# Ordering the experts by token count and halving the rows of fifteen of them in a fused transformer kernel

## The reference, cut to what matters

```
logits = hf @ router_w + router_b            # 512 x 32
top_val, top_idx = top_k(logits, 4); gate = softmax(top_val)
# every (token, expert) pair becomes a row of its expert's block(s) of 128 rows
u = hf[toks] @ w1[e] + b1[e]                 # 1024 -> 2048
g_ = minimum(u[:, :1024], 7);  lin = clip(u[:, 1024:], -7, 7)
y = ((lin + 1) * g_ * sigmoid(1.702 * g_)) @ w2[e] + b2[e]
out[token] += y * gate                       # four rows for each token
```

## Time and profile before

| | |
|---|---|
| device time, median of 3 runs | 3612.74 us (3610.33 to 3614.78) |
| span of the profiled execution | 3608.3 us |
| what lies around the span, against the median | 4.4 us |
| PE busy / DVE / ACT / GpSimd, share of the span | 93% / 80% / 39% / 20% |
| DMA, mean over the span | 307 GB/s |
| main steps of the expert stage | 30, about 498 to 1587 us of the span |

### The profile page before, as it was taken

The page is one execution under the profiler, slowest core; times in us unless marked ns, Lnnn a source line. Parts: engine busy times, 40 slices in busy tenths (PEclk is TensorE's granted clock), DMA queues, the critical chain, the costliest instruction groups (busy, mean ns, idle before and its releaser), DMA issues. The chain is left out here.

```text
span 3608.3 us, 39584 instructions
## 1 busy us (share of the span) xinstructions
PE 3345.7 (93%) x13996; PEld 2292.9 (64%) x13996; DVE 2896.8 (80%) x4756; ACT 1400.6 (39%) x1740; POOL 715.6 (20%) x720
## 2 busy tenths in 40 slices
PE   7999999999999999999999999988888888888876
PEld 4878767878787777775877787644443444434432
DVE  5777689999999999995995474688888888888886
ACT  2235357777777777773232452111111111111110
POOL 0001000000000000001000100244444444444442
PEclk9999999999999999999999999999999999999999
DMA  7422189999999999994224113899999999999998
GB/s 274 161 83 100 35 322 372 372 381 371 383 370 382 369 384 369 384 371 173 95 82 140 47 50 116 339 401 421 421 417 415 414 411 408 422 420 407 415 421 343
DMA packets 253815, 1105.96 MB, mean 307 GB/s; under 512 B 21137, under 2 KB 30737, under 8 KB 187793
## 3 DMA queue, kind: packets, MB, share of 16 engines
q1 hardware_dynamic: 166322, 521.20, 39.7%
q0 software_dynamic: 80640, 562.07, 38.0%
q10 hardware_dynamic: 6720, 20.97, 1.4%
HBM read 1071.15 MB, written 33.03 MB: 306 GB/s over the span
## 5 line engine op out<-in xcount | busy, mean ns | idle before, releaser
L1796 DVE TENSOR_TENSOR moe_w_lo<-ring,moe_w_hi 128x2048 fp32r<-128x2048 f32 x383 | 859.3, 2286 | 37.9 <-ACT moe_w_hi L1704 37.9
L1704 ACT ACTIVATE moe_w_hi<-ring 128x2048 fp32r<-128x2048 f32 x380 | 706.5, 1913 | 107.2 <-DMA ring<-in_exp_w 78.2
L2538 PE MATMUL last_banks<-last_rows_b,ring 128*128 128x512 f32 x1024 | 510.2, 646 | 121.7 <-DVE ring L2738 121.5
L2538 PE MATMUL last_banks<-last_rows_a,ring 128*128 128x512 f32 x1024 | 476.5, 609 | 85.4 <-DVE ring L2738 85.1
L2630 ACT ACTIVATE last_gelu<-last_dot 128x2 f32<-128x2 f32 (+1 forms) x257 | 52.3, 203 | 1118.9 <-DVE last_dot L2735 1118.8
L2538 PEld LDWEIGHTS last_banks<-last_rows_b,ring 128*128 128x128 f32 x1024 | 201.5, 205 | 403.5 <-issue 216.1
L2538 PEld LDWEIGHTS last_banks<-last_rows_a,ring 128*128 128x128 f32 x1024 | 188.6, 193 | 327.4 <-issue 201.1
L2417 POOL DMA_INDIRECT last_rows_a<-in_peer_uv,last_ids x256 | 279.9, 1093 | 501.2 <-PE last_banks L2538 318.7
L2417 POOL DMA_INDIRECT last_rows_b<-in_peer_uv,last_ids x256 | 294.9, 1152 | 390.2 <-PE last_banks L2538 365.5
L1550 POOL COPY moe_col<-slots 128x1 uint32 x31 | 51.4, 1658 | 959.7 <-PE moe_tp L1578 959.7
L2738 DVE TENSOR_SCALAR ring<-consts_sb,last_gelu,last_gates 128x128 f32<-128x128 f32 x512 | 161.6, 387 | 76.9 <-ACT last_gelu L2630 76.0
(11 more groups left out here) (506 smaller groups left out, 6530.5 us busy)
## 6 DMA issues: line engine op xcount, KB each, us to landing
ring<-in_exp_w SPq DMA_DIRECT2D x384, 1024.0 KB, 7.3
ring<-in_w_in SPq DMA_DIRECT2D x38, 1024.0 KB, 5.4
...
y_rows<-spare SPq DMA_DIRECT2D x1, 7680.0 KB, 25.4
...
```

Source lines behind the costliest of these rows:

```text
L1704: nc.scalar.activation(w_hi[:, slot, :], env.ring[:, slot, :], ACT.Copy).then_inc(hi_done, 1)
L1796: nc.vector.tensor_tensor(w_lo[:, slot, :], env.ring[:, slot, :], w_hi[:, slot, :].bitcast(F32), ALU.subtract).then_inc(lo_done, 1)
L2538: last = nc.tensor.matmul(sums(t)[:, q, :], diag[:, n % SL], slot(n)[:, D + q * W:D + (q + 1) * W], start=first, stop=final)
```

## The change

Experts are ordered by row count in the chip's routing code. Expert 0 keeps place 0; the others are ranked, and places 0, 2, 4, ..., 30 and 31 (17 of them) get the largest, places 1, 3, ..., 29 (15 of them, "small") the smallest. `expert_at` holds the expert of each place, and SyncE reads it to address the weights. A small place holds 64 rows; an expert with more there would overflow to the extra blocks. The half of each small block of `y_rows` that nothing writes is filled from `x` beforehand.

For a small expert, the 64 rounded rows and the 64 rests stand side by side as one stationary operand of 128 columns (`xt_hi_b`, `hidt_hi`), so that hi and lo rows are done by one pass: 8 matmuls for a chunk in place of 12. PSUM then has the rounded rows' sums in partitions 0 to 63 and the rests' in 64 to 127. To add them, ACT copies the bank to SBUF (`g_part`, `l_part`, `y_part`) and PE adds it back, shifted by 64 partitions, with 2 matmuls by `to_first`. The rests times `w_lo`, which were left out before, are computed too.

The gate is done in three DVE passes: ACT's sigmoid reads the unclipped PSUM bank, DVE computes min(g, 7) * sigmoid in one pass from PSUM, the 1 of (lin + 1) is added to the bias beforehand, and the product is bounded by `GATED_MAX`.

The order of chunks in a step from a small to a full expert becomes g, l, y; from a full to a small one it stays g, y, l. The first and the last main step stand outside the loop, which runs 14 times.

In the routing stage (SyncE's fill, then DVE), and SyncE's loads in the expert stage:

```diff
+unused = m["y_dram"][0:N_EXP * P, :].rearrange("(g f r) n -> f g r n", f=4, r=HALF)[3]
+some_rows = d["x"].rearrange("(g r) n -> g r n", r=HALF)
+for g0, g1 in ((0, 8), (8, N_EXP // 2 - 1)):
+    sp.dma_start(unused[g0:g1], some_rows[0:g1 - g0]).then_inc(filled, 16)
...
+chain(nc.vector.scalar_tensor_tensor(tie[:], cps, float(N_EXP), tie[:], ALU.mult, ALU.add))
+chain(nc.vector.tensor_tensor(before_it[:], tie[:].unsqueeze(1).to_broadcast([P, N_EXP, N_EXP]), tie[:].unsqueeze(2).to_broadcast([P, N_EXP, N_EXP]), ALU.is_gt))
+chain(nc.vector.tensor_reduce(order[:], before_it[:], AX, ALU.add))
+chain.also(nc.vector.tensor_scalar(nb[:], cps, float(P), None, ALU.is_gt))
+chain.also(nc.vector.tensor_scalar(small[:], order[:], N_FULL - 0.5, None, ALU.is_gt))
+chain(nc.vector.tensor_scalar(base[:], order[:], N_FULL - 1.5, -float(P), ALU.is_gt, ALU.mult))
+chain.also(nc.vector.scalar_tensor_tensor(limit[:], cps, float(HALF), small[:], ALU.is_gt, ALU.mult))
+chain(nc.vector.scalar_tensor_tensor(base[:], order[:], float(2 * P), base[:], ALU.mult, ALU.add))
 for j in range(2, NT):
     chain(nc.vector.scalar_tensor_tensor(nb[:], cps, float(j * P), nb[:], ALU.is_gt, ALU.add))
+chain.also(nc.vector.scalar_tensor_tensor(base[:], small[:], -float(N_EXP * P), base[:], ALU.mult, ALU.add))
+chain(nc.vector.tensor_tensor(nb[:], nb[:], limit[:], ALU.add))
+chain.also(nc.vector.tensor_scalar(limit[:], small[:], -float(HALF), float(P), ALU.mult, ALU.add))
...
+chain.also(nc.vector.tensor_tensor(past[:], rps, wide(limit), ALU.is_ge))
 chain(nc.vector.tensor_tensor(over[:], bend[:], nb[:], ALU.subtract))
+chain(nc.vector.tensor_tensor(over[:], over[:], small[:], ALU.add))
...
+chain(nc.vector.tensor_tensor(at_place[:], base[:].unsqueeze(1).to_broadcast([P, N_EXP, N_EXP]), starts[:].unsqueeze(2).to_broadcast([P, N_EXP, N_EXP]), ALU.is_equal))
+chain(nc.vector.tensor_tensor(at_place[:], at_place[:], iota[:, 0:N_EXP].unsqueeze(1).to_broadcast([P, N_EXP, N_EXP]), ALU.mult))
+chain(nc.vector.tensor_reduce(expf[:], at_place[:], AX, ALU.add))
+chain(nc.vector.tensor_copy(m["expert_at"][:], expf[:]))
+chain(nc.vector.tensor_scalar(m["row_pick"][:, 0:N_EXP], expf[:], env.const("expert_of_row"), None, ALU.is_equal))
...
+    e_now, e_next = expert(i), expert(i + 1)
     for j, (kind, n) in enumerate(kinds):
         sp.wait_ge(used, 12 * i + j + 1)
-        load_chunk(env, sp, i + 1 if kind != "y" else i, kind, n, slot_of(par, j), landed)
...
+        load_chunk(env, sp, e_next if kind != "y" else e_now, kind, n, slot_of(par, j), landed)
```

On PE:

```diff
+def few_chunk(s, slot, n, both, bank):
+    pe.wait_ge(lo_done, s + 1)
+    for a in range(2):
+        k = 2 * n + a
+        for w in (w_hi, w_lo):
+            for q in range(2):
+                last = nc.tensor.matmul(bank[:, q, :], both[:, k, :], w[:, slot, a * D + q * W:a * D + (q + 1) * W],
+                                        start=k == 0 and w is w_hi, stop=k == KC - 1 and w is w_lo)
+    last.then_inc(used, 1)
+def add_part(part, bank):
+    for q in range(2):
+        last = nc.tensor.matmul(bank[:, q, :], to_first[:], part[:, q * W:(q + 1) * W], start=False, stop=True, skip_group_check=True)
+    return last
...
+def to_small(i, n_small, first=False):
+    b = i + 1
     pe.wait_ge(x_lo, b * 2 + 2)
     pe.wait_ge(glu_done, b)
     for j in range(4):
-        chunk(at(i, j), slot_of(par, j), j, xt[u], glu_ps)
+        few_chunk(at(i, j), slot_of(0, j), j, xt[1][0], glu_ps)
         if j == 1:
+            if not first:
+                pe.wait_ge(y_parted, n_small)
+                add_part(y_part, yp).then_inc(y_done, 1)
             turn_hidden(i)
     pe.wait_ge(pick_ready, b + 1)
-    bias(glu_ps, u, 0).then_inc(g_done, 1)
     pe.wait_ge(h_lo, b * 2)
     pe.wait_ge(y_moved, b)
     for j in range(4):
-        chunk(at(i, 4 + j), slot_of(par, 4 + j), j, hidt, yp)
+        chunk(at(i, 4 + j), slot_of(0, 4 + j), j, hidt, yp)
         if j == 0:
             turn_rows(b + 1)
+        if j == 1:
+            pe.wait_ge(g_parted, n_small + 1)
+            bias(glu_ps, 1, 0, True)
+            add_part(g_part, glu_ps).then_inc(g_done, 1)
     pe.wait_ge(lin_done, b)
     for j in range(4):
-        chunk(at(i, 8 + j), slot_of(par, 8 + j), j, xt[u], lin_ps)
-    bias(lin_ps, u, FF).then_inc(l_done, 1)
+        few_chunk(at(i, 8 + j), slot_of(0, 8 + j), j, xt[1][0], lin_ps)
+def from_small(i, n_small, few_next=True):
+    b = i + 1
+    pe.wait_ge(x_lo, b * 2 + 2)
+    pe.wait_ge(glu_done, b)
+    for j in range(4):
+        chunk(at(i, j), slot_of(1, j), j, xt[0], glu_ps)
+        if j == 1:
+            pe.wait_ge(l_parted, n_small + 1)
+            bias(lin_ps, 1, FF, True)
+            add_part(l_part, lin_ps).then_inc(l_done, 1)
+    pe.wait_ge(pick_ready, b + 1)
+    bias(glu_ps, 0, 0).then_inc(g_done, 1)
+    pe.wait_ge(lin_done, b)
+    for j in range(4):
+        chunk(at(i, 4 + j), slot_of(1, 4 + j), j, xt[0], lin_ps)
+        if j == 0:
+            turn_few_hidden(i)
+        if j == 1 and few_next:
+            turn_few_rows(b + 1)
+    bias(lin_ps, 0, FF).then_inc(l_done, 1)
+    pe.wait_ge(h_lo, b * 2)
+    pe.wait_ge(y_moved, b)
+    for j in range(4):
+        few_chunk(at(i, 8 + j), slot_of(1, 8 + j), j, hidt[0], yp)
+        if j == 0 and not few_next:
+            turn_rows(b + 1)
```

On ACT:

```diff
+def glu_part(b, chunks):
+    act.wait_ge(used, chunks)
+    act.wait_ge(glu_done, b)
+    nc.scalar.activation(g_part[:], flat(glu_ps), ACT.Copy).then_inc(g_parted, 1)
+def lin_part(b, chunks):
+    act.wait_ge(used, chunks)
+    act.wait_ge(h_turn, b * 2)
+    nc.scalar.activation(l_part[:], flat(lin_ps), ACT.Copy).then_inc(l_parted, 1)
+def rows_part(b, chunks):
+    act.wait_ge(used, chunks)
+    act.wait_ge(stored, b * 16 + 16)
+    nc.scalar.activation(y_part[:], flat(yp), ACT.Copy).then_inc(y_parted, 1)
+def few_rows_out(b, n_small):
+    act.wait_ge(y_done, n_small + 1)
+    nc.scalar.activation(y[0:HALF], flat(yp, HALF), ACT.Copy).then_inc(y_moved, 1)
+    act.wait_ge(y_moved, b + 2)
+    act.dma_start(y_dram[span(b * P, HALF), :], y[0:HALF]).then_inc(stored, 16)
...
+def to_small(i, eights, n_small, first=False):
 
     b = i + 1
     for j in range(12):
-        round_chunk(slot_of(par, j), (three + (8 + 12 * par + j) // SL + 1) * 16)
...
+        round_chunk(slot_of(0, j), (eights + (8 + j) // SL + 1) * 16)
+        if j == 2 and not first:
+            rows_part(i - 1, at(i, 0))
+        if j == 4:
             round_hidden(i)
+            if not first:
+                few_rows_out(i - 1, n_small - 1)
+        if j == 6:
+            glu_part(b, at(i, 4))
         if j == 8:
+            round_rows(b + 1, 0)
+        if j == 9:
+            gate_of(b, HALF)
+    rows_out(i, at(i, 8))
+def from_small(i, eights, few_next=True):
+    b = i + 1
+    for j in range(12):
+        round_chunk(slot_of(1, j), (eights + (20 + j) // SL + 1) * 16)
+        if j == 2:
+            lin_part(i, at(i, 0))
+        if j == 7:
+            round_few_hidden(i)
             gate_of(b)
-            round_rows(b + 1, par)
...
+        if j == 9 and few_next:
+            round_few_rows(b + 1)
```

On DVE:

```diff
-def clip_glu(b):
...
-    nc.vector.tensor_scalar(glu[:], glu_ps[:].rearrange("p q n -> p (q n)"), 7.0, None, ALU.min).then_inc(glu_done, 1)
...
-def gate_glu(b):
+def gate_glu(b, rows=P):
     dve.wait_ge(sig_done, b + 1)
-    nc.vector.tensor_tensor(glu[:], glu[:], sig[:], ALU.mult).then_inc(gated, 1)
...
+    nc.vector.scalar_tensor_tensor(glu[0:rows], flat(glu_ps, rows), GLU_MAX, sig[0:rows], ALU.min, ALU.mult).then_inc(glu_done, 1)
+def hidden(b, rows=P):
     dve.wait_ge(l_done, b + 1)
-    nc.vector.tensor_scalar(lin[:], lin_ps[:].rearrange("p q n -> p (q n)"), 7.0, -7.0, ALU.min, ALU.max).then_inc(lin_done, 1)
+    nc.vector.tensor_scalar(lin[0:rows], flat(lin_ps, rows), GLU_MAX + 1.0, 1.0 - GLU_MAX, ALU.min, ALU.max).then_inc(lin_done, 1)
     dve.wait_ge(lin_done, b + 1)
...
-    nc.vector.scalar_tensor_tensor(lin[:], lin[:], 1.0, glu[:], ALU.add, ALU.mult).then_inc(hid_done, 1)
...
+    dve.wait_ge(glu_done, b + 1)
+    nc.vector.scalar_tensor_tensor(lin[0:rows], glu[0:rows], GATED_MAX, lin[0:rows], ALU.min, ALU.mult).then_inc(hid_done, 1)
...
+def to_small(i, first=False):
 
     b = i + 1
...
+    pick_row(b, 1, HALF)
     for j in range(12):
-        rest_of_chunk(at(i, j), slot_of(par, j))
...
+        rest_of_chunk(at(i, j), slot_of(0, j))
+        if j == 0 and first:
             hidden(i)
...
+        if j == 4:
             rest_of_hidden(i)
...
-            clip_glu(b)
         if j == 8:
...
+            rest_of_rows(b + 1, 0)
+        if j == 10:
+            gate_glu(b, HALF)
+def from_small(i, few_next=True):
+    b = i + 1
+    pick_row(b, 0)
+    for j in range(12):
+        rest_of_chunk(at(i, j), slot_of(1, j))
+        if j == 3:
+            hidden(i, HALF)
+        if j == 7:
+            rest_of_few_hidden(i)
+        if j == 8:
             gate_glu(b)
+        if j == 9 and few_next:
```

(39 more changed lines are left out.)

150 lines of the change are left out of this document (98 added, 52 removed).

## The result

The changed kernel takes 3532.38 us (median of 4 runs, 3523.86 to 3535.16) against 3613.25 us (4 runs, 3610.33 to 3614.78): ratio 0.9768, 95% interval 0.9757 to 0.978, 80.9 us less. The forecast was 3560, in a range of 3522 to 3612; the direction and the bound hold, and the gain is 28 us larger than forecast. The profiled execution took 3535.16 us, its span is 3533.3: 1.9 us lie around the span, as in every run that lists both. The 4.4 us in the table of the kernel before are not that; its profiled execution, of span 3608.3, thus took near 3610.2, faster than its median.

The account below looks back on a forecast made before the run. PE was taken as the bound before, DMA after: 15 pairs of steps from 72.4 to 68.2 us save 63 us, the head adds 10.7, so -52.5 from 3612.7 gives 3560 us; range of 8 in 10, 3522 to 3612.

Parts of the forecast that it names:

- PE: Expert stage, matmul engine: bound of the kernel before; one small and one full expert fall from 72.4 to 62.6 us.
- DVE: Expert stage, vector passes: two steps fall from 67.8 to 64.3 us through two passes and two 512-column instructions fewer.
- DMA: Expert stage, loads, gathers and stores: 67.9 us for two steps (67.0 to 68.7), largest sum, taken as 68.2.
- the disturbance of the 128-row gather: Queues behind each full gather: 285 in place of 414 GB/s for 5.5 us, a cost of 1.7 us.
- slow stretch of half the length behind the small gather: Sign in the steady steps: after a 64-row gather the queues slow for half as long; disturbance taken as 0.85 us.
- GpSimd's index copy: Index copy beside the experts: 1.66 us on the mean, and 0.18 at its first, read as with DVE idle.
- ACT: Expert stage: three bank copies of 1.03 us added, 55.8 of 68.2 us for two steps; no cost taken.
- Head: Routing ahead of the experts: 8.7 us more serial DVE work and 2 for PE's low clock, +10.7 in sum.
- The list of signs: What the trace should show, including gathers 68.2 us apart and the first expert matmul 9 us later in the span.
- A: Rival: loads already at their ceiling of 377 GB/s, so only saved bytes count; 10 us less, 3602; chance 0.13.
- B: Rival: DMA gives way and DVE bounds the expert stage at 66.3 us a pair; 80 less, 3532; chance 0.22.
- C: Rival: ACT's in-order part copies stall the roundings, 79.2 us a pair; slower, 3725; chance 0.12.

Follow-up runs that it names:

- The first run: The kernel before with the three-pass gate alone, no ordering and no 64-row blocks: 3607.61 us, ratio 0.9996 against the kernel before.

## Why the prediction was right, and where it was off

**PE.** Right: the bound goes away from PE. 63.6 us a pair against 62.6; 42 matmuls fewer a pair, as counted. Where the 1.0 us more comes from isn't shown.

**DVE.** Right: 64.2 against 64.3. Its 1.9 us below the pair are no cost, as the run with a pass less shows; but 2.35 us of DVE more cost 2.65 a pair. The first run shows the other side, nothing saved under a busy PE. With PE 63.6, DVE 64.2 and DMA 66.1 the three limits stand close together: relief for PE alone gave 3.8 us of the 6.3 a pair, and the gate paid only with it.

**DMA.** The bound as forecast, and the term that was mis-sized. 26.74 MB a pair at 411 GB/s is 65.1 us; 411 is the mean rate from 12 to 20 us behind the 128-row gathers of the kernel after, well clear of them. I had added 1.7 us for the disturbance of the 128-row gather, 0.85 for the 64-row one and 0.3 for DVE; measured is 66.09 - 65.1 = 1.0 for all of it. The step that failed is the reading of the earlier trace rows: I took 285 GB/s over 5.5 us as the price of the gather. It was the price of a gather while PE lets only few loads into the queue (one or two in flight as it is issued, 7.5 us to a landing in the nine pairs before). With three in flight and 11.6 us to a landing the gather at 1038.58 costs 6 x (411 - 395) / 411 + 3 x (411 - 380) / 411 = 0.5 us, and the 64-row one 0.8; on the mean of ten it is 8 x (411 - 396) / 411 = 0.3 and 2 x (411 - 260) / 411 = 0.7, together the 1.0 measured. The runs with later loads bring the stretch back with the gather unchanged, and in the run with two products it comes and goes with the number in flight, in one kernel. 2.1 us x 15 pairs = 31 us, against 28 missed.

I had also forecast a slow stretch of half the length behind the small gather. There is none of the old kind at all; there is another, 2 us long and later, that the 128-row form doesn't have, and fetching 64 rows in place of 128 gained nothing.

**GpSimd's index copy.** I had read its 0.18 us as a copy with DVE idle. It was not: DVE had begun an instruction 0.03 us earlier, with one operand in PSUM and one in SBUF. Beside `w_lo` passes, which read two SBUF operands, the copy ends with the pass. The Trainium skill (SBUF — State Buffer, "SBUF: two separate sides") describes the ports that GpSimd and DVE share as a lock that one of them holds for a whole instruction, and names a DVE instruction with two SBUF inputs as a holder against a GpSimd instruction that reads SBUF. The trace agrees on the copy: 0.04 us behind the end of a pass, 29 times of 29. No run here shows whether such a lock bears on the gather itself.

**ACT.** Right: 54.4 against 55.8; its largest waits are for landings, and the list of its waits from 500 to 1600 us has none ahead of a part copy.

**Head.** +10.7 as forecast, but with terms that cancel: `slots` came 6.1 us later (4.4 forecast; between two runs with the same code up to there it moved by 1.3), from `slots` to the start of the stage 3.6 more (4.3), and from there to the first expert matmul 1.0 more, with the granted clock at 0.72 from 485 to 490 us and at 0.59 from 490 to 495, in place of 2. The list of signs had said 9 us for the whole, against 10.7 in the sum. The fill of `y_rows` and SyncE's reads of `expert_at` show no cost.

**The rivals.** A is refuted by 404 GB/s. B gave the measured time, 3532, with a pair of 66.3, and half of its condition came true (the faster chunks do keep the backlog). But its bound, DVE, is not the bound, so that it has the number is luck. The range reached down to it, and that is why the measured time lies inside. C did not come about.

The 358 GB/s for a core that the Trainium skill gives (DMA: Bandwidth & Descriptors, "Specifications") disagree with the kernel after as with the one before: it moves 404 over 595 us.
